# Single heads' states by token tiles of 128, and a third projection unit taken depth tile by depth tile in the opening

## The reference

```python
cum = cumsum(log_a, within a chunk)
q_rel, k_rel = q * exp(cum - cum_mid), k * exp(cum_mid - cum)
o_intra = where(causal, q_rel @ k_rel.T, 0) @ v
update = (k * exp(cum_last - cum)).T @ v          # one per chunk
state[n + 1] = exp(cum_last)[n] * state[n] + update[n]
o_inter = (q * exp(cum)) @ state[n]               # the state before the chunk
```

## Time and profile before

| what | value |
|---|---|
| median of 3 runs | 1164.52 us (1164.21 to 1164.85) |
| profiled execution | 1163.81 us |
| its span, first to last instruction | 1162.1 us |
| mean granted TensorE clock | 0.995 |
| busy: TensorE, VectorE, ScalarE, GpSimd | 98%, 74%, 53%, 43% of the span |

### The profile page before, as it was taken

The page is one execution under the profiler, slowest core; times in us unless marked ns, Lnnn a source line. Parts: engine busy times, 40 slices in busy tenths (PEclk is TensorE's granted clock), DMA queues, the critical chain, the costliest instruction groups (busy, mean ns, idle before and its releaser), DMA issues.

```text
span 1162.1 us, 15677 instructions
## 1 busy us (share of the span) xinstructions
PE 1135.4 (98%) x5555; PEld 939.4 (81%) x5555; DVE 865.3 (74%) x1044; ACT 612.4 (53%) x933; POOL 494.9 (43%) x320
## 2 busy tenths in 40 slices
PE   7999999989999999999999999999999999999996
PEld 7788788777878788888888888888888888788886
DVE  6898887587778677377976775677795884966876
ACT  7763555756566566255654555455664433524424
POOL 1021122134243345336534343344566675665751
PEclk9999999999999999999999999999999999999999
DMA  9777387344353546722445344544624637447203
GB/s 356 263 234 272 129 202 209 79 127 134 92 173 100 155 122 213 241 77 82 143 156 184 142 156 125 182 145 159 195 64 161 220 92 264 150 133 278 71 1 145
DMA packets 162949, 186.73 MB, mean 161 GB/s; under 512 B 7604, under 2 KB 119352, under 8 KB 159928
## 3 DMA queue, kind: packets, MB, share of 16 engines
q1 hardware_dynamic: 160472, 179.44, 46.7%
q0 software_dynamic: 2400, 6.29, 2.8%
HBM read 138.51 MB, written 40.89 MB: 154 GB/s over the span
## 4 chain that ended last, share of the span: by engine, by line
PE 92%; DVE 2%; DMA 2%; ACT 2%; SPq 1%; issue 1%; DVEq 0%; ACTq 0%
PE unit_bank L1764 19%; PE unit_bank L2178 9%; PE unit_bank L2180 9%; PE unit_bank L2179 9%; PE small_bank L2178 9%; PE small_bank L2180 9%; PE small_bank L2179 9%; PE small_bank L1764 4%; PE unit_bank L2025 3%; PE unit_bank L2027 3%; PE unit_bank L2026 3%; PE small_bank L1901 2%; DMA ada_slot<-in_w_ada_dram 2%; PE small_bank L1803 1%; PE small_bank L1893 1%
## 5 line engine op out<-in xcount | busy, mean ns | idle before, releaser
L1016 POOL TENSOR_TENSOR wr_lo<-quarter,wr_hi 128x512 fp32r<-128x512 f32 x122 | 197.2, 1628 | 174.6 <-ACT wr_hi L1552 174.4
L2178 PE MATMUL unit_bank<-op_hi,wr_hi 128*128 128x512 f32 x452 | 176.8, 391 | 0.9 <-issue 0.9
L2180 PE MATMUL unit_bank<-op_hi,wr_lo 128*128 128x512 f32 x452 | 176.0, 389 | 0.0
L2179 PE MATMUL unit_bank<-op_lo,wr_hi 128*128 128x512 f32 x452 | 176.0, 389 | 0.0
L2178 PE MATMUL small_bank<-op_hi,wr_hi 128*128 128x512 f32 x448 | 174.6, 390 | 0.0
L2179 PE MATMUL small_bank<-op_lo,wr_hi 128*128 128x512 f32 x448 | 174.4, 389 | 0.0
L2180 PE MATMUL small_bank<-op_hi,wr_lo 128*128 128x512 f32 x448 | 174.4, 389 | 0.0
L1552 ACT ACTIVATE wr_hi<-wr_full 128x512 fp32r<-128x512 f32 x90 | 56.8, 631 | 174.8 <-DVE wr_full L2921 174.8
L2921 DVE TENSOR_TENSOR wr_full<-quarter,quarter 128x512 f32<-128x512 f32 x90 | 89.1, 991 | 56.8 <-PE small_bank L2180 22.9
L1552 ACT ACTIVATE wr_hi<-quarter 128x512 fp32r<-128x512 f32 x136 | 82.9, 626 | 89.3 <-PE unit_bank L2180 49.1
L1764 PE MATMUL unit_bank<-a_hi,w_hi 128*128 128x512 f32 x304 | 121.1, 398 | 0.0
(11 more groups left out here) (370 smaller groups left out, 2382.5 us busy)
## 6 DMA issues: line engine op xcount, KB each, us to landing
quarter<-in_w_mlp_dram SPq DMA_DIRECT2D x128, 256.0 KB, 4.1
hidden_scratch<-hid SPq DMA_DIRECT2D x98, 256.0 KB, 2.3
ada_slot<-in_w_ada_dram SPq DMA_DIRECT2D x48, 512.0 KB, 6.6
op_full<-hidden_scratch SPq DMA_DIRECT2D x21, 1024.0 KB, 4.8
pair_quarter<-in_w_in_dram SPq DMA_DIRECT2D x32, 256.0 KB, 3.6
piece_x<-t_scratch SPq DMA_DIRECT2D x16, 512.0 KB, 4.1
piece_y<-t_scratch SPq DMA_DIRECT2D x32, 256.0 KB, 3.4
raw<-in_w_out_dram SPq DMA_DIRECT2D x16, 512.0 KB, 3.9
```

Of the source, the lines that this page charges most:

```text
L1016: pool.tensor_tensor(wr_lo[slot][:, :, :], split_source(n), wr_hi[slot][:, :, :].bitcast(F32), ALU.subtract).then_inc(wr_lo_pool, 1)
L2178: pe.matmul(dst, wh, ah, start=opens, stop=False, skip_group_check=True)
L2179: pe.matmul(dst, wh, al, start=False, stop=False, skip_group_check=True)
L2180: mm = pe.matmul(dst, wl, ah, start=False, stop=k == KH - 1, skip_group_check=True)
```

## The change

Two parts.

*Single heads by tiles of 128 tokens.* The state is kept before each of 8 token tiles: 7 updates of 128 tokens (`update_tiles`), 7 state products of 128 tokens, 7 state steps on VectorE with `decay_tile`, the product of both chunks' decays. For that the first chunk's keys are scaled by the second chunk's decay (`far_keys`), the second chunk's queries by the first chunk's decay (`tile_queries`). What the second chunk sees of the first one was in the state before; now it is a score: an extra 64x64 product per tile of `k_near` (the first chunk's keys to its end) with `q_near` (the second chunk's queries), put in the unused quarter of the score bank, and the mask lets it through. TensorE turns `k_end` only when `far_keys` has run.

*The third unit.* Unit 2 (queries of the first GLA pair) gets the small banks 2 and 3, its own load into `w_full`, which GpSimd copies to `w_hi[0]`, and a high-with-high and high-with-low product in each of the first four depth tiles' loops. Its other products stand where the unit stood, the low-with-high ones of the first four depth tiles last. `pack_gate` and the low weights of unit 1 move one adaLN addition ahead. The low weights of unit 2 wait for the last `a_lo`.

```diff
     s = [[] for _ in range(10 if prev == "H" else 8)]
     if own == "P":
-        s[0] += [("z", 0, 0, 2), ("z", 0, 1, 3)]
+        s[0] += [("z", 0, 0, 2), ("z", 0, 1, 3)] if prev else [("z", 0, 0, 0), ("z", 0, 1, 1)]
...
-        s[1] += [("up", 0, 0, 2), ("up", 1, 0, 3)]
+        s[1] += [("up", 0, 0, 2)]
...
-        s[6] += [("up", 2, 1, 3), ("up", 3, 1, 0)]
+        s[6] += [("up", 1, 1, 3)]
...
             load_unit(1, 1, w_in, 0, GK)
             for n in range(8, 20):
                 load_ada(n)
+                if n == 8:
+                    sp.dma_start(w_full[:, :, :], w_in[0, :, GQ:GQ + P].rearrange("(k p) m -> p k m", p=P)).then_inc(gain_loaded, 16)
             pair_cols = [GQ, GV, GV + P, GK + P, GQ + P, GV + 2 * P, GV + 3 * P]
             head_cols = [HF, HQ, HI, GG]
             n = 20
             for j, q in enumerate(pair_cols + head_cols):
-                load_unit(2 + j, j % 2, w_in, 0, q)
+                if j:
+                    load_unit(2 + j, j % 2, w_in, 0, q)
                 if j == 6:
                     sp.wait_ge(read["x"], 16)
...
                 return blocks(t, k, half).bitcast(F32)
 
+            pool.wait_ge(whi_ready, 2)
+            pool.wait_ge(gain_loaded, 16)
+            pool.tensor_copy(w_hi[0][:, :, :], w_full[:, :, :]).then_inc(whi_ready, 1)
             for u in range(2, U_OUT):
+                if u == 2:
+                    pool.wait_ge(lo_dve, 16)
                 low(u, u % 2)
                 if u == 9:
...
             def high(u, slot, loads):
 
-                act.wait_ge(raw_loaded[slot], 16 * loads)
+                act.wait_ge(raw_loaded[slot], 16 * (loads - (u >= 2 and slot == 0)))
                 if not isinstance(u, int) or u >= 3:
                     act.wait_ge(unit_filled[1], u - 1)
...
+            def third_unit(half, tiles):
+
+                for k in tiles:
+                    wh, wl = w_hi[0][:, k, :], w_lo[0][:, k, :]
+                    ah, al = tok(a_hi[:, k], half), tok(a_lo[:, k], half)
+                    product(third_bank(half), wh, ah, k == 0, False)
+                    product(third_bank(half), wh, al, False, False)
+                    if k >= KH:
+                        pe.wait_ge(wlo_ready, 3)
+                        product(third_bank(half), wl, ah, False, False)
+
+            def third_unit_end(half):
+
+                pe.wait_ge(wlo_ready, 3)
+                for k in range(KH):
+                    mm = product(third_bank(half), w_lo[0][:, k, :], tok(a_hi[:, k], half), False, k == KH - 1)
+                mm.then_inc(unit_filled[half], 1)
...
+                if prev == "H":
+                    pe.wait_ge(q_cum_ready, gi)
+                    pe.wait_ge(k_far_ready, gi - 1)
                 for i in range(4):
                     for _, which, half, b, _ in pieces:
                         mine = rows_of(prev, which)
...
+                        if prev == "H":
+                            mm = product(SB[b][0:CH, i * P + CH:(i + 1) * P], k_near[:, 4 * half + i, :], q_near[:, 4 * half + i, :])
                         if i == 3:
                             mm.then_inc(filled["sc"], 1)
 
...
+                        for n in update_tiles(half):
+                            mm = product(SB[b][:, n % 4 * P:(n % 4 + 1) * P], k_nat[:, n % 4, :], v_nat[:, 0, n, :])
+                        mm.then_inc(filled["up"], 1)
+                    return
+                chunks = [update_chunks(which) for _, which, _, _, _ in pieces]
...
+                    b = pieces[0][3]
+                    for n in range(max(4 * half, 1), 4 * half + 4):
+                        mm = pe.matmul(SB[b][:, n % 4 * P:(n % 4 + 1) * P], state[:, n, :],
+                                       q_cum_of(gi - 1)[:, n * P:(n + 1) * P],
+                                       start=False, stop=n % 4 == 3, skip_group_check=True)
+                    mm.then_inc(filled["o"], 1)
...
+                        if k4 == 0:
+                            if k == 0:
+                                pe.wait_ge(whi_ready, 3)
+                                pe.wait_ge(read["ada"], half + 1)
+                            third_unit(half, (k,))
...
+                    if name == "P0" and j == 1:
+                        if half:
+                            third_unit(half, range(KH, KT))
+                        third_unit_end(half)
...
                 if n == 8:
                     finish_ada(0, 0, 2)
                     finish_ada(0, 1, 3)
-                if n == 9:
                     pack_gate()
...
+            def far_keys():
+
+                dve.tensor_tensor(chunk_of_tiles(k_end, 0), k_near[:, :, :], decay_of(1).broadcast_to([P, TT, CH]), ALU.mult
+                                  ).then_inc(k_far_ready, 1)
+
+            def tile_queries(dst, q, since, gi):
+
+                dve.wait_ge(decay_ready, gi + 1)
+                then(dve.tensor_tensor(decay_tile[:, :].rearrange("p (n i) -> p n i", i=1), decay_of(0), decay_of(1), ALU.mult), False)
+                then(dve.scalar_tensor_tensor(q_near[:, :, :], chunk_of_tiles(q, 1), 0.5, chunk_of_tiles(since, 1),
+                                              ALU.mult, ALU.mult), False)
+                dve.scalar_tensor_tensor(chunk_of_tiles(dst, 0), chunk_of_tiles(q, 0), 0.5, chunk_of_tiles(since, 0),
+                                         ALU.mult, ALU.mult)
+                dve.wait_ge(setup, chain[0])
+                dve.tensor_tensor(chunk_of_tiles(dst, 1), q_near[:, :, :], decay_of(0).broadcast_to([P, TT, CH]), ALU.mult
+                                  ).then_inc(q_cum_ready, 1)
+
...
                 read_out(4)
+                if own == "H":
+                    dve.wait_ge(read["sc"], before("sc", FIRST_PAIRED))
+                    then(dve.memset(causal[0:CH, CH:P], 1.0), False)
...
-                                         ).then_inc(q_cum_ready, 1)
+                if own == "H":
+                    tile_queries(q_cum, t0, cum, gi)
+                else:
+                    dve.scalar_tensor_tensor(q_cum[:, :], t0[:, :], factor, cum[:, :], ALU.mult, ALU.mult
+                                             ).then_inc(q_cum_ready, 1)
                 if name == "P1":
                     low_third()
                 if own == "H":
                     weight_sum_of(0, "S2")
+                    then(dve.tensor_copy(k_near[:, :, :], chunk_of_tiles(k_end, 0)))
+                    far_keys()
...
+                    b, place = at_["up", half]
+                    dve.wait_ge(filled["up"], before("up", gi) + place + 1)
+                    for n in update_tiles(half):
                         if n:
                             dve.wait_ge(read["up"], done + n)
-                        dve.scalar_tensor_tensor(state[:, n + 1, :], state[:, n, :], decay[:, n:n + 1],
-                                                 SB[at_["up", which][0]][:, place * P:(place + 1) * P], ALU.mult, ALU.add
+                        dve.scalar_tensor_tensor(state[:, n + 1, :], state[:, n, :], decay_tile[:, n:n + 1],
+                                                 SB[b][:, n % 4 * P:(n % 4 + 1) * P], ALU.mult, ALU.add
                                                  ).then_inc(read["up"], 1)
 
                 def low_squares(half):
...
                 dve.wait_ge(e_end, gi + 1)
-                dve.tensor_tensor(k_end[:, :], k_end[:, :], t1[:, :], ALU.mult).then_inc(k_end_ready, 1)
+                dve.wait_ge(filled["sc"], before("sc", gi + 1))
+                then(dve.tensor_tensor(k_near[:, :, :], chunk_of_tiles(k_end, 0), chunk_of_tiles(t1, 0), ALU.mult), False)
+                dve.tensor_tensor(chunk_of_tiles(k_end, 1), chunk_of_tiles(k_end, 1), chunk_of_tiles(t1, 1), ALU.mult
+                                  ).then_inc(k_end_ready, 1)
                 join(late, "11")
                 dve.wait_ge(read["up"], before("chunks", gi + 1))
                 dve.wait_ge(e_cum, gi + 1)
                 dve.tensor_copy(decay[:, :].rearrange("p (n c) -> p n c", c=1), chunked(own_cum)[:, :, CH - 1:CH]
                                 ).then_inc(decay_ready, 1)
                 dve.wait_ge(decay_ready, gi + 1)
+                dve.wait_ge(setup, chain[0])
+                far_keys()
                 dve.wait_ge(c_read["11"], C_READ_0["11"] + early + 1)
                 dve.wait_ge(c_read["12"], C_READ_0["12"] + early + 1)
-                dve.scalar_tensor_tensor(own_cum[:, :], q_rel[:, :], 0.5, own_cum[:, :], ALU.mult, ALU.mult).then_inc(q_cum_ready, 1)
+                tile_queries(own_cum, q_rel, own_cum, gi)
```

More of the change, by code:

```diff
@@ L386, in hybrid_layer @@
         decay = at("decay", 206.6875, [P, NC])
+        decay_tile = at("decay_tile", 206.65625, [P, TT])
+        k_near, q_near = at("k_near", 188.5, [P, TT, CH]), at("q_near", 190.5, [P, TT, CH])
         x_stat = at("x_stat", 206.6875, [P, TT])
@@ L930, in low @@
                 pool.wait_ge(whi_ready, u + 1)
```

(36 more changed lines are left out.)

54 lines of the change are left out of this document (29 added, 25 removed).

## The result

The changed kernel took 1180.1 us (median of 4 runs, 1179.4 to 1182.8), the kernel before beside it 1164.7. The ratio is 1.013 (1.012 to 1.015): 15.5 us slower. The forecast was 1162.7, the range ended at 1167.3, and its slowest rival gave 1168.7. The profiled execution took 1182.8 us with a span of 1181.1, so it stands 2.7 us above the median and 19.0 above the profiled execution of before. Its mean granted clock, 0.988, is the lowest of the four (0.990 to 0.992 in the others), so its sums show more of the clock than the median has.

What follows compares the result with a forecast made beforehand. TensorE was taken as the bound, busy 98% of the span with 92% of the last chain. Opening +0.65, first single head +1.0, paired groups -2.2, last head -1.3 sum to -1.85 us: 1162.7 us, range 1159.2 to 1167.3.

Steps and rivals of the forecast that it cites:

- its slowest rival: Whole kernel: the granted clock falls behind new stalls in all four places, +4.2 us, 1168.7; chance 0.14.
- the near score: Each single head: eight added k_near with q_near products at 0.15 us each, +1.2 us a head (0.97 to 1.78).
- the VectorE chain of the paired groups: From P4's joins to the second sq_lo, over VectorE and ScalarE: 1.0 us shorter (-1.5 to +0.5).
- H0: First single head's states: q_cum becomes several instructions ahead of ScalarE's tanh, +1.0 us, all on the path (0.6 to 1.3).
- G: Last head, without the six squares' stalls: TensorE's whole saving of 1.3 us arrives.
- Opening: Third unit's products moved into the first loops: -0.15 us, plus 0.8 for GpSimd's copy to w_hi, together +0.65.
- the step I am surest of: Opening: the fourth unit waits 1.6 us for its banks, so of 1.81 us gained only 0.15 to 0.2 remain.
- TensorE's own work: Each head: outputs -1.85 us, updates -0.6, added near scores +1.2, net -1.3 (-1.5 to -0.7).
- The paired groups: Three groups computing two pairs: gain is how much earlier the chain ends, -1.0, -0.6, -0.6, together -2.2 us (-4.5 to +2.5).
- X: Paired groups: TensorE starts the chain +1.0 us later; nearly all taken up in the first group, 0.6 at join "21".
- the clock, which I had as a rival with 0.14: Opening and three paired groups: clock granted at 0.50 behind new stalls, 1.5 us lost in each; chance 0.14.

Runs made afterwards that it cites:

- e1: The kernel before with the opening's part of the change alone, heads as before: 1166.8 us, ratio 1.0019.
- e3: The changed kernel with each score step's four near products grouped behind its four full ones, no longer alternating: 1175.0 us, ratio 1.0082.
- e7: The changed kernel with near products of 128 columns of weights in place of 64, still alternating, near scores not computed: 1175.6 us, ratio 1.0089.
- e11: The kernel before with the opening's part, the second z product early, and two conditioning-row additions moved behind the k_end product: 1168.3 us, ratio 1.0031.
- e9: The changed kernel without near products, and with VectorE's preparation of keys and queries in the paired groups put back to plain: 1161.2 us, ratio 0.9975.
- e4: The changed kernel with the near products left out and that quarter of the scores kept closed: 1167.0 us, ratio 1.0019.
- e2: The changed kernel with the opening's part undone: 1179.0 us, ratio 1.0118.
- e10: The kernel before with VectorE's added work alone, four 128x512 instructions per paired group ahead of q_cum: 1177.8 us, ratio 1.0123.
- e5: The kernel before with the second low part of the squares moved ahead of the queries with their sums: 1167.5 us, ratio 1.0024.
- e6: The changed kernel with the second low part of the squares moved ahead of far keys, queries and sums: 1180.3 us, ratio 1.0128.
- e8: The kernel before with the opening's part alone and the second z product moved ahead of three depth tiles: 1167.2 us, ratio 1.0018.

## Why the prediction was wrong

Two terms carry most of the miss: the near score, taken at 0.15 us and measured at 0.46, and the VectorE chain of the paired groups, taken as 1.0 us shorter and measured as long as before. TensorE's lag behind the kernel before, read at the same product in both profiles, is +2.0 us ahead of H0's stall, +3.0 at the first near scores (241.83 before), +7.4, +11.9 and +17.2 behind the three paired groups (at 285.71, 338.74 and 391.87 before) and +19.0 behind G.

**Opening (+0.65 forecast, +2.4 measured).** Up to the fourth unit the account came out. In e1, from the first product behind a_lo to the fourth unit's first it is 33.99 us (36.04 to 70.03), before 34.13 (35.92 to 70.05): -0.14, and -0.15 was forecast, with the wait of 1.57 us where 1.6 was. GpSimd's copy took 1.71 us, longer than the 1.0 to 1.6 allowed, and costs 0.5 us, not 0.8: from the start of the addition at 29.87 to the first a_lo at 35.09 it is 5.2 us before, and 5.7 after (29.39 to 35.11); so it is in the other profiles, 5.2 in all four without the copy and 5.7 in eight of the nine with it (6.1 in the ninth). The two a_lo starts alone don't show it, since that addition could start 0.5 us earlier in the execution after. The rule of the Trainium skill (SBUF - State Buffer, on the shared port pair) is not contradicted: two VectorE additions beside and behind that copy took 3.01 us where 2.5 was due. The 0.8 to 1.2 worked out by it was too much.

The failed step is that the account stops at "the step I am surest of". It took only the first late link. The same delay reached the fifth unit too (a wait of 0.73 at 82.61; in e1 the lag goes from 0.0 to +1.0 there), because VectorE, which runs between, was full; its idle time at the gate's low part is 1.8 us in the changed kernel and 0.5 in the one before. By the transposes at 91.89 another 0.3 us had come. That makes 0.5 - 0.1 + 1.0 + 0.3 = 1.7 us; the other 0.7 of the 2.4 stays open, within e1's interval (1.0 to 3.3 us). In its profile the longer fall of the clock behind H0's stall would cover it, but the mean clocks of all executions (0.994 to 0.995, and 0.992 to 0.996 before) don't show such a difference. The changed kernel's profile has 0.8 us more, from the fall of the clock at 37 us (34.75 us in place of 33.99 to the fourth unit).

**H0 (+1.0, measured +0.9).** Right. The stall at k_nat grew from 3.46 to 4.17, and TensorE's lag from 2.0 to 2.9 us.

**TensorE's own work (forecast -1.3 a head).** Outputs and updates came as priced: 0.21 to 0.22 for each product of 128 rows, -2.45 a head. The failed term is the near score: "I take 0.15", with 0.22 as upper bound. Measured 0.46, so eight cost 3.7 us a head and not 1.2, and a head gets 1.2 us dearer instead of 1.3 cheaper. The bounds came from rows of products that follow their like. No row before showed two sizes of weights in turn, and I did not count that as unknown. e3 and e7 show that it is this alternation that broke the bound. The rule quoted from the Trainium skill (TensorE: Matmul & The Clock Gate, on LDWEIGHTS), that loading goes by the number of weight columns, would have made it 0.11 each; the runs contradict that use of it, since 128 columns alternating with 128 are cheaper than 64 with 128. The loads' own records do go that way, 0.19 us for the two of a near product and 0.30 for the two of a full one; the spacing of the products does not.

**The paired groups (-1.0, -0.6, -0.6, measured +4.4, +4.5, +5.3 by the lag).** Three steps failed. X, by which the scores move the chain's start, was +1.0 and is about +3.5; nor did other waits take it up in the first group, which lost 4.4. "Chain: -1.0" was 0: from the end of P4's products to the second squares 25.3 us before (303.3 to 328.64) and 25.2 after (314.3 to 339.52). The timeline of VectorE in the second part, with one line of GpSimd's, after:

```profile
325.88 1.31 DVE L2854 TENSOR_TENSOR t<-q_cum 128x1024 f32<-128x1024 f32 x1
...
330.02 1.87 POOL L991 TENSOR_TENSOR pw_lo<-pw_full,pw_hi 128x512 fp32r<-128x512 f32 x1 [3.90 <-ACT pw_hi L1359]
...
330.65 1.79 DVE L2865 TENSOR_TENSOR k_near<-k_end,t 128x512 f32<-128x512 f32 x1
332.36 0.68 DVE L2866 TENSOR_TENSOR k_end<-k_end,t 128x512 f32<-128x512 f32 x1
...
334.26 0.69 DVE L2528 TENSOR_TENSOR k_end<-k_near,decay 128x512 f32<-128x512 f32 x1
334.87 0.16 DVE L2534 TENSOR_TENSOR decay_tile<-decay 128x8 f32<-128x8 f32 x1
334.95 0.69 DVE L2535 SCALAR_TENSOR_TENSOR q_near<-q_rel,q_cum 128x512 f32<-128x512 f32 x1
335.55 0.69 DVE L2537 SCALAR_TENSOR_TENSOR q_cum<-q_rel,q_cum 128x512 f32<-128x512 f32 x1
336.16 0.68 DVE L2540 TENSOR_TENSOR q_cum<-q_near,decay 128x512 f32<-128x512 f32 x1
...
338.69 0.69 DVE L2799 TENSOR_TENSOR sq_lo<-stat,sq_hi 128x512 fp32r<-128x512 f32 x1
```

and the same part before:

```profile
316.58 1.22 DVE L2759 TENSOR_TENSOR t<-q_cum 128x1024 f32<-128x1024 f32 x1
...
321.25 1.22 DVE L2769 TENSOR_TENSOR k_end<-k_end,t 128x1024 f32<-128x1024 f32 x1
...
323.69 2.27 DVE L2778 SCALAR_TENSOR_TENSOR q_cum<-q_rel,q_cum 128x1024 f32<-128x1024 f32 x1
...
327.81 0.69 DVE L2704 TENSOR_TENSOR sq_lo<-stat,sq_hi 128x512 fp32r<-128x512 f32 x1
```

From VectorE's first line to its last: 11.2 us before, 12.8 after, +1.6. What lies ahead of it got shorter by as much. The states brought their 1.5, and the preparation took 1.6: the two halves of the k_end product cost 2.3 us (330.65 to 332.97) where the whole took 1.1 (321.25 to 322.38), so +1.2 and not +0.1. The 2.27 us of q_cum did vanish, but k_near's 1.79 took its place as the one that stands beside a GpSimd subtraction (330.02 to 331.89). So TensorE's saving behind the outputs went whole into the stall (3.2 to 3.6 in place of 0.9), while the added scores ahead of P4 were paid in full.

The third is the clock, which I had as a rival with 0.14, at 1.5 us in each of four places. It came in all three groups and took 6.1 us of this profile there. In the fourth place, the wait of 1.57 us at 70.69, it did not come. It came at 37 us, behind the wait of 1.89 us, which the prediction doesn't name and which e1 and e11 have without a fall.

**The last head, G (-1.3, measured +1.8).** The near score is again the term, and G got a stall of its own at the squares, 1.01 us at 435.88, where the prediction let the whole saving arrive.

**The ledger.** Opening +2.4 (e1). States by tiles with the preparation plain -5.6 (e9 against e1; forecast 4 x 2.45 = 9.8, while idle time and clock take 6.4 us more over 240 to 450 than in e1). Preparation +5.8 (e4 against e9). Near products +8.0 in a row and +5.2 for the alternation. Sum +15.8, measured 15.5; since each term is a difference of neighbouring kernels, the sum has to come out near the total and is no evidence by itself. Nothing between them points to a version faster than the one before: what the near products need may cost no more than 5.6 - 2.4 = 3.2 us with the opening, or 5.6 without. Grouped they cost 8.0, and the preparation that makes their operands another 5.8. What holds the stalls of 1.2 to 2.6 us that remain in e9 was not tried.

## What to carry to other kernels

Where TensorE already waits for a chain of another engine, sum what the change adds to that engine's queue in that stretch before counting any saving on TensorE; a stall that moves when the order is changed, with the same idle sum, belongs to the queue and not to the operation that shows it. Price a new small product by a row of its own neighbourhood: between products of another shape it can cost several times what it costs among its like. And where a new stall arises, count the lower clock behind it as a second price: behind the stalls of over 3 us in the paired groups it was 1.7 to 3 us each, behind shorter ones 1.7 us or nothing.

## What the runs showed of the hardware

- Products with 128x128 weights alternating with products with 128x64 weights took 0.67 us a pair (fp32, two records each); grouped by size the near ones took 0.15 each; alternating at equal size a pair took 0.45.
- The length of a stall did not alone decide on the clock. The grant fell to 0.50 at each of the 15 stalls of 3.2 to 3.6 us in the paired groups (after, e2, e3, e7, e10), and also behind 1.66 (e5, 287.29) and 2.02 us (e9, 328.70), for 3.4 or 6.8 us each time; it stayed at 1.00 behind 1.57 (after, 70.69), 2.25 (e6, 283.43), 2.42 (e8, 83.21), 2.45 (e11, 93.58) and 2.56 us (e9, 259.41). The same wait for the first a_lo, 1.89 to 1.90 us, was followed by a fall in two profiles (after, e8) and by none in two others (e1, e11). What tells them apart is open.
- A GpSimd cast of 128x1024 took 1.71 us at 31.02 where one of 128x256 took 0.40. Two VectorE additions beside and behind it took 3.01 us where 2.5 was due.
